# Inverse roots token by token, the first two tiles behind a norm together, and the first norm's shift and scale in two halves

## The reference, cut to what matters

```python
cond = jax.nn.silu(c)
for layer in range(2):
    mod = cond @ ada_w[layer] + ada_b[layer]
    sh_m, sc_m, g_m, sh_f, sc_f, g_f = jnp.split(mod, 6, axis=-1)
    h = rms_norm(x) * (1.0 + sc_m) + sh_m
    x = x + g_m * mixer(h)
    h = rms_norm(x) * (1.0 + sc_f) + sh_f
    x = x + g_f * peer_ffn(h)
return rms_norm(x, final_norm)       # x * rsqrt(mean(x * x) + 1e-6)
```

## Time and profile before

| | us |
|---|---|
| median of 3 runs (lowest, highest) | 3599.19 (3589.68, 3601.59) |
| profiled execution, own time | 3586.02 |
| its span | 3584.2 |
| PE busy | 3463.3 (97%) |
| DVE busy | 2604.0 (73%) |
| ACT busy | 1767.7 (49%) |
| POOL busy | 1120.5 (31%) |

### The profile page before, as it was taken

One profiled execution on the slowest core, in us unless ns is written; L12 is line 12 of the kernel. 1 busy time (PEld: TensorE's weight loads), 2 busy tenths in 40 slices (PEclk: granted clock), 3 DMA queues, 4 the chain that ended last, 5 costly groups with the idle time before them and its releaser, 6 DMA issues.

```text
span 3584.2 us, 62733 instructions
## 1 busy us (share of the span) xinstructions
PE 3463.3 (97%) x19978; PEld 3144.9 (88%) x19978; DVE 2604.0 (73%) x4761; ACT 1767.7 (49%) x3216; POOL 1120.5 (31%) x852
## 2 busy tenths in 40 slices
PE   7988999999999999998999999899999999999998
PEld 5545799999999999997776688689999999999997
DVE  2654668579996888886887644585669996888886
ACT  3354445557884333335774133345557875333333
POOL 2100442434441222222664002343444442222221
PEclk8999999999999999999999999999999999999999
DMA  7654245799999999993457452235698999999995
GB/s 241 210 166 141 73 140 172 235 331 333 381 377 370 359 345 350 344 345 105 156 172 209 131 161 78 80 114 174 198 342 302 375 376 365 368 348 347 345 349 192
DMA packets 519774, 914.08 MB, mean 255 GB/s; under 512 B 70256, under 2 KB 359152, under 8 KB 511216
## 3 DMA queue, kind: packets, MB, share of 16 engines
q1 hardware_dynamic: 445936, 644.23, 52.4%
q0 software_dynamic: 73728, 268.47, 21.0%
HBM read 782.54 MB, written 130.02 MB: 255 GB/s over the span
## 4 chain that ended last, share of the span: by engine, by line
PE 87%; ACT 5%; DMA 3%; DVE 3%; issue 1%; SPq 0%; POOL 0%; DVEq 0%; ACTq 0%; POOLq 0%
PE bank L736 11%; PE bank L738 11%; PE bank L737 11%; PE bank L808 10%; PE bank L810 10%; PE bank L809 10%; PE bank L784 5%; PE bank L446 3%; PE bank L956 2%; PE bank L965 1%; PE bank L539 1%; PE bank L747 1%; DMA w_ring<-b_w_in 1%; PE bank L1030 1%; PE bank L1032 1%
## 5 line engine op out<-in xcount | busy, mean ns | idle before, releaser
L736 PE MATMUL bank<-hx,hl 128*128 128x384 f32 (+1 forms) x2304 | 798.0, 346 | 0.8 <-POOL hl L1512 0.8
L738 PE MATMUL bank<-hx,hl 128*128 128x384 f32 (+1 forms) x2304 | 785.7, 341 | 0.0
L737 PE MATMUL bank<-hx,hl 128*128 128x384 f32 (+1 forms) x2304 | 785.5, 341 | 0.0
L808 PE MATMUL bank<-W,hl 128*128 128x384 f32 x2048 | 688.8, 336 | 6.2 <-DVE W L2558 6.2
L810 PE MATMUL bank<-W,hl 128*128 128x384 f32 x2048 | 688.4, 336 | 0.0
L809 PE MATMUL bank<-W,hl 128*128 128x384 f32 x2048 | 688.3, 336 | 0.0
L1535 POOL DMA_INDIRECT rows<-p_v,erow x256 | 262.0, 1024 | 850.8 <-DVE xtok L2565 828.8
L1535 POOL DMA_INDIRECT rows<-p_u,erow x256 | 356.6, 1393 | 405.1 <-DVE rows L2491 367.2
L1840 ACT ACTIVATE hl<-hT 128x1024 fp32r<-128x1024 f32 x272 | 287.8, 1058 | 358.1 <-PE bank L810 303.4
L1840 ACT ACTIVATE hl<-w_ring 128x1024 fp32r<-128x1024 f32 x272 | 287.6, 1058 | 342.7 <-PE bank L810 304.7
L736 PEld LDWEIGHTS bank<-hx,hl 128*128 128x128 f32 x2304 | 434.6, 189 | 10.5 <-POOL hl L1512 1.0
(11 more groups left out here) (355 smaller groups left out, 5411.0 us busy)
## 6 DMA issues: line engine op xcount, KB each, us to landing
w_ring<-p_u_t SPq DMA_DIRECT2D x128, 512.0 KB
hT<-p_u_t SPq DMA_DIRECT2D x128, 512.0 KB
w_ring<-p_v SPq DMA_DIRECT2D x128, 512.0 KB
hT<-p_v SPq DMA_DIRECT2D x128, 512.0 KB
act_scratch<-hT SPq DMA_DIRECT2D x256, 192.0 KB
g_scratch<-gst SPq DMA_DIRECT2D x48, 1024.0 KB
gg<-g_scratch SPq DMA_DIRECT2D x64, 768.0 KB
ua<-act_scratch SPq DMA_DIRECT2D x256, 192.0 KB
```

Source lines behind the costliest of these rows:

```text
L736: nc.tensor.matmul(bank[s][:, c:], hi, hx[:, 0, k, c:], start=(k == 0), stop=False)
L737: nc.tensor.matmul(bank[s][:, c:], hi, hx[:, 1, k, c:], start=False, stop=False)
L738: mm = nc.tensor.matmul(bank[s][:, c:], lo, hx[:, 0, k, c:], start=False, stop=(k == KD - 1))
L808: nc.tensor.matmul(bank[j][:, P:], hi, W[:, s, 0, :], start=first, stop=False)
```

## The change

- The squares are no longer multiplied by a matrix of ones. `sums` makes, of each block, the four groups of 128 x 128 squares the stationary operand and one column of ones the moving one: four matmuls of one column, into four columns of bank 2. The sums then lie with tokens on the partitions, and ACT's root and DVE's reciprocal work on 128 x 4 numbers (`root`).
- `spread` puts the inverse roots back over all partitions: four matmuls of 128 columns (`root` broadcast, times the identity) into bank 2. DVE multiplies `xT` by bank 2 directly, and frees bank 2 only after all eight blocks.
- In norm4 DVE does the gain too, and ACT has no part in it.
- In PEER and DeltaNet the first two tiles are done together, block by block.
- The first norm's shift and scale are made in two halves of the features: chunks 0 and 2 first, ACT goes on with blocks 0 to 3, then the rest.

```diff
+        root = sb("root", [P, TT])
...
+        def ada_chunk(n):
+            return {1: 2, 2: 1}.get(n, n)
...
+                    col = 4 * ada_chunk(n) + c
+                    mm = nc.tensor.matmul(bank[3][:, col:col + 1], ada_part[:, n % 2, c * P:(c + 1) * P],
                                           ones[:, 0:1], start=True, stop=True)
                 return mm
...
+            def sums(k, first, last):
+                for q in range(TT):
+                    mm = nc.tensor.matmul(bank[2][:, q:q + 1], hT[:, k, q * P:(q + 1) * P], ones[:, 0:1],
+                                          start=(first and q == 0), stop=(last and q == TT - 1))
+                if last:
+                    mm.then_inc(psum_full[2], 1)
+            def spread(stage):
+                pe.wait_ge(sem("root_ready"), int(stage[-1]) + 1)
+                take(2)
+                for q in range(TT):
+                    mm = nc.tensor.matmul(bank[2][:, q * P:(q + 1) * P], root[:, q:q + 1].to_broadcast([P, P]), ident[:, :],
+                                          start=True, stop=True)
+                mm.then_inc(psum_full[2], 1)
+                mark(stage)
+                marks[stage][2] -= 2
...
                 take(2)
                 pe.wait_ge(sem("squares_added"), (KD - 2) * times)
-                nc.tensor.matmul(bank[2][:, :], ones[:, :], hT[:, 0, :], start=True, stop=False)
+                sums(0, True, False)
                 pe.wait_ge(sem("squares"), t.turn("squares", KD) + KD)
-                nc.tensor.matmul(bank[2][:, :], ones[:, :], hT[:, KD - 1, :], start=False, stop=True
-                                 ).then_inc(psum_full[2], 1)
-                mark(stage)
-                marks[stage][2] -= 1
+                sums(KD - 1, False, True)
+                spread(stage)
...
-                for n in range(4):
-                    ada_rows(n)
-                    if n > 0:
-                        ada_columns(n - 1)
+                ada_rows(0)
+                ada_rows(1)
+                ada_columns(0)
+                ada_columns(1).then_inc(sem("mods_in"), 1)
+                ada_rows(2)
+                ada_rows(3)
+                ada_columns(2)
                 ada_columns(3).then_inc(psum_full[3], 1)
...
-            def add_square(k):
-                if k == 0:
-                    take(2)
-                pe.wait_ge(sem("squares"), t.turn("squares") + 1)
-                mm = nc.tensor.matmul(bank[2][:, :], ones[:, :], hT[:, k, :], start=(k == 0), stop=(k == KD - 1))
-                if k == KD - 1:
-                    mm.then_inc(psum_full[2], 1)
             def norm(stage):
+                take(2)
                 for k in range(KD):
-                    add_square(k)
-                mark(stage)
-                marks[stage][2] -= 1
+                    pe.wait_ge(sem("squares"), t.turn("squares") + 1)
+                    sums(k, k == 0, k == KD - 1)
+                spread(stage)
...
-                def split_product(s, c=P, by_block=False):
+                def split_product(s, c=P):
...
-                        if by_block:
-                            turn_input(k)
...
+                def first_pair():
+                    for s in range(2):
+                        pe.wait_ge(sem(f"split_done{s}"), t.turn(f"split{s}") + 2)
+                        take(s)
+                    for k in range(KD):
+                        turn_input(k)
+                        for s in range(2):
+                            hi, lo = hl[:, s, 0, k, :], hl[:, s, 1, k, :]
+                            nc.tensor.matmul(bank[s][:, :], hi, hx[:, 0, k, :], start=(k == 0), stop=False)
+                            nc.tensor.matmul(bank[s][:, :], hi, hx[:, 1, k, :], start=False, stop=False)
+                            mm = nc.tensor.matmul(bank[s][:, :], lo, hx[:, 0, k, :], start=False, stop=(k == KD - 1))
+                            if k == KD - 1:
+                                mm.then_inc(psum_full[s], 1)
...
-                        split_product(s, 0, by_block=first and s == 0)
+                        if first and s == 0:
+                            first_pair()
+                        elif not first or s > 1:
+                            split_product(s, 0)
...
-                        if n == 0:
-                            pe.wait_ge(sem("hx_ready"), 2 * KD + k + 1)
...
-                head_tile(0)
+                for n in range(2):
+                    pe.wait_ge(sem(f"split_done{n}"), t.turn(f"split{n}") + 2)
+                    take(n)
+                for k in range(KD):
+                    pe.wait_ge(sem("hx_ready"), 2 * KD + k + 1)
+                    for n in range(2):
+                        high, low = head_weights(n)
+                        nc.tensor.matmul(bank[n][:, :], high[:, k, :], hxg[:, 0, k, :], start=(k == 0), stop=False)
+                        nc.tensor.matmul(bank[n][:, :], high[:, k, :], hxg[:, 1, k, :], start=False, stop=False)
+                        mm = nc.tensor.matmul(bank[n][:, :], low[:, k, :], hxg[:, 0, k, :], start=False, stop=(k == KD - 1))
+                        if k == KD - 1:
+                            mm.then_inc(psum_full[n], 1)
                 pe.wait_ge(sem("gdn_params"), 80)
                 narrow_rows(7, w_beta[:, :, :])
                 narrow_columns(7, sq[:, 0, :], 2 * VH)
-                head_tile(1)
...
-                sp.dma_start(ada_slot(n), ada_w[l, :, j * T:(j + 1) * T].rearrange("(k p) c -> p k c", p=P)
+                sp.dma_start(ada_slot(n), ada_w[l, :, ada_chunk(j) * T:(ada_chunk(j) + 1) * T].rearrange("(k p) c -> p k c", p=P)
...
-            def modulations():
-                sync("mod")
-                for n in range(4):
-                    ada_out(n)
-                in_high(0)
-                in_high(1)
-                act.wait_ge(sem("mods_ready"), 1)
-            def norm(stage, gain=None, l=0, sh=0, sc=0, split=None, x_block=None, prelude=None, ahead=None):
+            def modulations(half):
+                if half == 0:
+                    sync("mod")
+                ada_out(2 * half)
+                ada_out(2 * half + 1)
+                if half == 0:
+                    act.wait_ge(sem("mods_half"), 1)
+                else:
+                    in_high(0)
+                    in_high(1)
+                    act.wait_ge(sem("mods_ready"), 1)
+            def norm(stage, l=0, sh=0, sc=0, split=None, x_block=None, prelude=None, ahead=None):
...
-                nc.scalar.activation(rstd[:, :], bank[2][:, :], ACT.Sqrt, scale=1.0 / D, bias=eps[:, 0:1]
+                nc.scalar.activation(root[:, :], bank[2][:, 0:TT], ACT.Sqrt, scale=1.0 / D, bias=eps[:, 0:1]
                                      ).then_inc(psum_free[2], 1)
+                t.turn(2)
                 if stage == "norm0":
-                    modulations()
+                    modulations(0)
...
-                for k in range(KD):
+                for k in range(KD if split is not None else 0):
+                    turned = stage == "norm0" and k == KD // 2
+                    if turned:
+                        high_of_input(k - 1)
+                        modulations(1)
                     act.wait_ge(sem("hn_ready"), t.turn("hn") + 1)
-                    if gain is None:
-                        ins = nc.scalar.activation(hT[:, k, :], hT[:, k, :], ACT.Identity,
-                                                   bias=mods[:, l, sh + k:sh + k + 1], scale=mods[:, l, sc + k:sc + k + 1])
-                    else:
-                        ins = nc.scalar.activation(hT[:, k, :], hT[:, k, :], ACT.Copy, scale=gain[:, k:k + 1])
-                    if split is not None:
-                        ins.then_inc(sem("act_step"), 1)
-                        if k > 0:
-                            high_of_input(k - 1)
-                    else:
-                        ins.then_inc(sem("h_ready"), 1)
+                    ins = nc.scalar.activation(hT[:, k, :], hT[:, k, :], ACT.Identity,
+                                               bias=mods[:, l, sh + k:sh + k + 1], scale=mods[:, l, sc + k:sc + k + 1])
+                    ins.then_inc(sem("act_step"), 1)
+                    if k > 0 and not turned:
+                        high_of_input(k - 1)
...
-                step(nc.vector.reciprocal(rstd[:, :], rstd[:, :]))
+                nc.vector.reciprocal(root[:, :], root[:, :]).then_inc(sem("root_ready"), 1)
+                full(2)
+                if to is None:
+                    for k in range(KD):
+                        nc.vector.scalar_tensor_tensor(hT[:, k, :], xT[:, k, :], fnorm[:, k:k + 1], bank[2][:, :],
+                                                       ALU.mult, ALU.mult).then_inc(sem("h_ready"), 1)
+                    return
...
-                    nc.vector.tensor_tensor(hT[:, k, :], xT[:, k, :], rstd[:, :], ALU.mult).then_inc(sem("hn_ready"), 1)
-                    if to is not None and k >= behind:
```

(38 more changed lines are left out.)

1 line of the change is left out of this document (removed).

## The result

The changed kernel takes 3619.0 us (median of 11 runs, 3610.4 to 3637.6), the kernel before 3597.6 beside it (11 runs, 3582.5 to 3607.9). The ratio is 1.0071, with a 95% interval from 1.0053 to 1.0088: slower by 19 to 32 us, where 21.8 were forecast. The profiled execution has a span of 3619.0 us and a time of 3620.74 of its own; the granted clock over the span is 0.986 for 0.990.

A forecast was written before the change was run, and what follows sets the result against it. TensorE, busy 97%, bounds the kernel, with waits at the five norms; 7.3 + 5.6 + 6.0 + 0.6 + 2.3 = +21.8 us takes the median from 3599.2 to 3621.0 us, own range 3609 to 3631 (3597 to 3632 with rival (1)).

The forecast's parts named there:

- The column sums lose the clock: One-column matmuls on TensorE lose the high clock as a gap does; the stage behind starts low for 4 to 5 us.
- rival (1): All norms: column sums don't cost the clock; +4.9 us, 3604, no change that can be told; chance 0.20.
- norm0: First norm to first tile's end: low-clock sums and a new wait for bank 2; +7.3 us, bounds +0.8 to +11.
- norm1: Second norm to third tile: fourth late chunk waits for bank 2; +5.6 us, bounds +2 to +7.
- norm2: Third norm to narrow product: sums +4.3, root, reciprocal and spread to +2.6, pair +3.4; +6.0 us in all.
- my bound of +8: High bound at norm2: the clock gone at once and 7 us to recover.
- The pair's +3.4: Before norm2's narrow product, which now waits for both tiles: 13.1 us where one tile took 9.7.
- norm3: Fourth norm, as norm1 without late rows: pairs start earlier but run partly at low clock; +0.6 us, bounds -1.4 to +1.5.
- norm4: Last norm: +2.6 as in norm2, ACT's step -0.6, bank reads 0.5; +2.3 us, bounds -2.9 to +4.
- Rival (2): All norms: shorter root and reciprocal pass on whole, 5 x 2.64 = -13.2 us, 3586; chance 0.06.
- Rival (3): DVE's product from a bank is held behind POOL too: norm1 +2.6, norm3 +2.9 more; +27.3 us, 3626.5; chance 0.10.
- The sum: All five norms together: +21.8 us; low bounds make -2.8, high ones +31.5.

The follow-up runs named there:

- The roots alone: The kernel before with token-by-token roots in all five norms, without pairs or the two-halves shift and scale; ratio 1.0037 (1.0024 to 1.0051).
- the two kernels that show it alone: Kernel before plus both pairs: ratio 1.0016; changed kernel with the second DeltaNet head tile back behind the narrow product: ratio 1.0055.
- the last version: Kernel before plus halves and token-by-token roots in all norms, sums except norm3's over 128 columns, first chunk in bank 6, fourth late chunk in bank 1; ratio 0.9940.
- the halves alone: The kernel before with the first norm's shift and scale made in two halves of the features, nothing else; ratio 0.9995 (0.9980 to 1.0009).
- the one with the pairs alone: The kernel before with the first two query tiles paired and the first two DeltaNet head tiles paired, nothing else; ratio 1.0016 (1.0000 to 1.0033).

## Why the prediction was right, step by step

- **The column sums lose the clock, and rival (1) falls.** This was the deciding step, and it was taken from thin evidence, one fall in `late_columns`: these 32 matmuls keep the high level to the end or nearly so in nine of the fourteen kernels (3.62 to 3.80 us), and lose it sooner in five (4.13 to 4.85). The 64 of norm2 lost it in all five kernels that have them. The windows of norm2 show it, and the sums over 128 columns prove it: with the columns restored the clock holds, and norm2 and norm4 together are 10 us better (in the table, +8.5 and +1.4 become +2.2 and -2.7).
- **norm0, +7.3 forecast, +5.5 measured.** Sums of 14.1 forecast, 13.79 measured; the wait for bank 2 was there, to 34.13 for the 33.7 forecast, and moving the bank gave 4.4 us back. The rows of the first two chunks took 4.99 us together, less than the 6.2 I had.
- **norm1, +5.6 forecast; +4.1 at the third tile, +5.0 at the third scores.** The first product is not held (0.63 us), the subtraction is; the fourth chunk waits for bank 2. But the hole was 2.75 us and not 7, because the clock was lost already behind this norm's two blocks of column sums (it is 0.50 from 368.0, and the spread took 2.08 us for the 1.05 I took), so that the three earlier chunks ran into the hole's time. I had it high there, as it was in three kernels of seven. The roots alone kept it, had the hole of 5.79, and lost 3.0: either way the gain of the root is gone.
- **norm2, +6.0 forecast, +8.5 measured, above my bound of +8.** The mis-sized term is the sums: 11.5 us forecast, with three blocks at the high clock, 13.0 measured; the fall came in the first 4 us. (In the four other kernels with these sums they take 11.4 to 13.0 us, so the forecast was not far from the usual.) The pair's +3.4 was 4.0 and 4.1 in the two kernels that show it alone; that the second tile's removal from its old place gains nothing was right too.
- **norm3, +0.6 forecast, +1.0 at the third tile, +1.9 at the third scores.** It is the difference of two terms that I should have priced apart: -2.9 for the root, the only norm where it pays as built, and +5.0 for the pair.
- **norm4, +2.3 forecast, +1.4 measured**: +3.5 for the sums, where I had +4.3, -2.1 for root, reciprocal and the fused gain. (The terms as I wrote them, 2.6 - 0.6 + 0.5, add up to 2.5.)
- **Rival (2)**, the shorter chain passing on, was wrong for the change as built. With the clock kept in the sums, no bank held and no pairs it comes near: norm1 to norm4 give 12.5 us by the local spans of the last version, where this rival had 10.6 for the four. The 21.6 us of its ratio hold the halves as well.
- **Rival (3)** is refuted by the product's 0.63 us.
- **The sum**: +21.8 forecast, +22.2 by local spans, +21.4 by the medians, +25.5 (19 to 32) by the ratio. That it is so close is luck: the terms are off by -1.8, -0.6, +2.5, +1.3 and -0.9 us and cancel. The sign was right at every norm, and what stands in the way was named rightly at norm0, norm2 and norm4; at norm1 and norm3 in part, as said above.

I had not seen how the parts act on one another. Alone, the halves save 5.6 us at the first tile; beside the new roots 2.2 (58.08 for 60.29), because rows, columns and copies then come late. And a gain at norm0 must pass the attention, which differs by some 3 us between executions of the same code; that of the halves alone did not show behind it.

## What to carry to other kernels

A reduction by one-column matmuls looks cheaper than it is: each still loads 128 columns of weights, and a stretch of them can cost TensorE its high clock for the stage behind it (each time with the 64 records of norm2, some times with 32 or 16). With 128 moving columns, as many as the weight load has, the sums here took no longer and kept the clock. When a product starts to read a PSUM bank where it read SBUF, ask which TensorE instruction writes that bank next: it waits for the last reader, and everything behind it on TensorE waits with it (5.12, 2.75 and 5.79 us here). And pair tiles only if TensorE has room within the pace of the inputs; else the pair delays what frees the buffer that the next load needs.

## What the runs showed of the hardware

**With 128 columns of weights to load, a 128-column matmul costs what a one-column one does.** 0.116 us a record against 0.114 at the high clock, above; neither rows of before nor the forecast had this.

**The long PEER product runs at one of two paces, at the same granted clock.** Windows of 30 us within the down product of the second PEER stage, of the kernel before and then of the changed one, where no instruction differs:

```profile
3141.22:3171.22 30.00, 30.00 (x176) 1.00 0.95 339
3201.22:3231.22 30.00, 30.00 (x175) 1.00 0.97 349
```

```profile
3163.21:3193.21 30.00, 30.00 (x172) 1.00 0.94 343
3223.21:3253.21 30.00, 30.00 (x172) 1.00 0.96 339
```

TensorE is busy throughout and ends 175 or 176 matmuls or 172, which over the 3072 matmuls that this product has in a stage makes an estimated 9 to 12 us. From the third scores to the last update of x a stage takes 1242 to 1249 us, or 1255 to 1258, in either PEER stage and with the changed code or without it: the kernel before had 1243 and 1245, the changed one 1246 and 1257, the one with the pairs alone 1244 and 1256, the fastest version 1246 and 1257. The two stages together are 14.5 us longer in the profiled execution of the changed kernel, which is about what its difference of 34.8 us from before has over the 21.4 of the medians, and why I read the norms by local spans. What sets the pace I don't know.
